# Constant products in four waits of TensorE, and three changes of order, in a two-layer diffusion step

## The reference, cut to what matters

```python
m = silu(cond) @ w_ada[l] + b_ada[l]                  # 6 vectors of 1024 per condition
h = x * (1 + m[1]) + m[0];  proj = h @ w_in[l]
s = q1 @ k1.T, q2 @ k2.T;  pd = softmax(s1) - lam * softmax(s2);  o_a = rms_norm(pd @ v)
mixed = concat([o_a, o_b, o_c])                       # 512 + 256 + 256 columns
x = layer_norm(ALPHA * x + m[2] * (mixed @ w_out[l]), ln_g[0], ln_b[0])
h = x * (1 + m[4]) + m[3]
y = moe_ffn(h)          # sigmoid router, best group, top 2 of its 4 experts; silu(h wg) * (h wu) @ wd
x = layer_norm(ALPHA * x + m[5] * y, ln_g[1], ln_b[1])
```

## Time and profile before

| | us |
|---|---|
| timed runs: median (lowest to highest) of 3 | 2076.75 (2075.97 to 2078.27) |
| the profiled execution | 2085.36 |
| its span, first to last instruction | 2083.5 |
| its mean granted TensorE clock | 0.936 of 2.4 GHz |

### The profile page before, as it was taken

The page is one execution under the profiler, slowest core; times in us unless marked ns, Lnnn a source line. Parts: engine busy times, 40 slices in busy tenths (PEclk is TensorE's granted clock), DMA queues, the critical chain, the costliest instruction groups (busy, mean ns, idle before and its releaser), DMA issues. The chain is left out here.

```text
span 2083.5 us, 20602 instructions
## 1 busy us (share of the span) xinstructions
PE 1809.4 (87%) x7528; PEld 927.7 (45%) x7528; DVE 755.3 (36%) x1179; ACT 374.4 (18%) x695; POOL 310.7 (15%) x348
## 2 busy tenths in 40 slices
PE   3999999788956999999799999988798399999983
PEld 1464555554443443434345445554545243443431
DVE  0036567374462110111060575746636310110105
ACT  1323122243010000000141422213411000000002
POOL 0001266000000000000130223630000000000005
PEclk9999999899977999999899999998998599999996
DMA  9421111565019687799603012136121696797934
GB/s 364 151 98 41 36 54 46 207 238 194 21 51 364 251 328 291 286 358 379 220 38 125 13 46 84 47 132 222 54 75 42 249 348 233 294 357 299 393 124 151
DMA packets 142086, 380.43 MB, mean 183 GB/s; under 512 B 9732, under 2 KB 15876, under 8 KB 135332
## 3 DMA queue, kind: packets, MB, share of 16 engines
q1 hardware_dynamic: 111840, 292.31, 37.5%
q10 hardware_dynamic: 21108, 55.36, 7.5%
q0 software_dynamic: 9040, 31.46, 4.1%
HBM read 343.65 MB, written 35.45 MB: 182 GB/s over the span
## 5 line engine op out<-in xcount | busy, mean ns | idle before, releaser
L855 PE MATMUL psum<-sb_arena 128*128 128x512 f32 (+1 forms) x1248 | 494.1, 596 | 10.6 <-DMA sb_arena<-w_up 9.1
L583 PE MATMUL psum<-sb_wA,sb_arena 128*128 128x512 f32 x800 | 365.3, 605 | 0.9 <-DMA sb_wA<-w_in 0.9
L855 PEld LDWEIGHTS psum<-sb_arena 128*128 128x128 f32 (+1 forms) x1248 | 192.5, 171 | 269.7 <-issue 257.7
L855 PE MATMUL psum<-sb_wA,sb_arena 128*128 128x512 f32 (+1 forms) x672 | 278.4, 611 | 9.3 <-DMA sb_wA<-w_up 6.6
L583 PEld LDWEIGHTS psum<-sb_wA,sb_arena 128*128 128x128 f32 x800 | 147.5, 192 | 165.3 <-issue 158.0
L1329 DVE TENSOR_TENSOR sb_arena<-sb_arena 128x320 f32<-128x320 f32 (+8 forms) x252 | 170.8, 719 | 13.4 <-POOL sb_arena L1264 3.8
L1849 DVE COPY sb_arena<-psum 128x1024 f32<-128x1024 f32 x32 | 39.2, 1225 | 344.3 <-PE psum L843 344.3
L855 PEld LDWEIGHTS psum<-sb_wA,sb_arena 128*128 128x128 f32 (+1 forms) x672 | 103.3, 170 | 120.2 <-issue 109.7
L1495 DVE COPY_PREDICATED sb_arena<-sb_masks,psum 128x640 f32<-128x640 uint8 x128 | 112.4, 878 | 90.8 <-PE psum L656 71.5
L574 PE MATMUL psum<-sb_arena,sb_wA 128*128 128x128 f32 (+1 forms) x512 | 140.4, 435 | 0.0
L815 PE MATMUL psum<-sb_wA,sb_arena 128*128 128x512 f32 x320 | 140.3, 599 | 0.0
(11 more groups left out here) (184 smaller groups left out, 1685.1 us busy)
## 6 DMA issues: line engine op xcount, KB each, us to landing
sb_arena<-w_gate SPq DMA_DIRECT2D x22, 2048.0 KB, 18.5
sb_arena<-w_down SPq DMA_DIRECT2D x22, 2048.0 KB, 15.8
sb_wA<-w_up SPq DMA_DIRECT2D x16, 2048.0 KB, 19.4
sb_arena<-w_up SPq DMA_DIRECT2D x16, 2048.0 KB, 15.5
sb_wA<-w_ada SPq DMA_DIRECT2D x13, 2048.0 KB, 7.7
sb_wA<-w_in SPq DMA_DIRECT2D x12, 2048.0 KB, 9.6
sb_arena<-w_ada SPq DMA_DIRECT2D x11, 2048.0 KB, 7.6
sb_wA<-w_gate SPq DMA_DIRECT2D x10, 2048.0 KB, 18.0
```

The costliest lines, as they stand in the source:

```text
L583: mm = pe.matmul(unit_bank(n), hT[:, k, t * P:(t + 1) * P], w[:, k, :], start=k == 0, stop=k == KD - 1)
L855: mm = pe.matmul(out[r, :], act_T[:, k, r], w[:, k, cs], start=k == 0, stop=k == kn - 1)
```

## The change

Four edits, in both layers unless said:

1. `HALVES`: half pieces 0 to 3 are done after the scores of heads 0 and 1 and before the wait for head 0; heads 1 to 18 have one each, head 19 the last two.
2. `stay_warm(b, n)`: n products of the identity with 512 constant columns into bank 2, whose result nobody reads: 6 before the wait for `m_ready`, 11 before `at_ready`, 8 before the first block's tokens, 5 before `pos_ready`.
3. `mix_ready` is raised once per tile. TensorE turns tiles 0 and 1 once `oa_evac` and `row_sum` are complete, tile 2 behind the projection of tile 0 and tiles 3 and 4 behind that of tile 1. ACT's three loads now stand behind the evacuation of tile 1 and a wait for all five tiles.
4. Last norm of layer 1: ACT sums x and its squares (two passes with `accum_out`), POOL computes mean, variance, power and bias in six small operations, ACT normalises, DVE multiplies by g and adds b, two tiles behind its residual. The wait for the rows g and b (`ln2_in`) moves ahead of the first tile, in both layers.

```diff
-HALVES = [range(n + (n + 1) // 5 - (n % 5 == 4), n + 1 + (n + 1) // 5) for n in range(20)]
+HALVES = [range(4)] + [range(n + 3, n + 4) for n in range(1, 19)] + [range(22, 24)]
...
+            def stay_warm(b, n):
+                for _ in range(n):
+                    pe.matmul(bank(b), ident, cst[:, 0:W], start=True, stop=True)
...
                     if n + 1 < 20:
                         scores(n + 1)
+                    if n == 0:
+                        for h_ in HALVES[0]:
+                            row_products(h_)
                     pe.wait_ge(pd_ready, nth(l, 20, n + 1))
...
-                pe.wait_ge(mix_ready, l + 1)
-                for t in range(NT):
+                def turn_mixed(t):
+                    pe.wait_ge(mix_ready, nth(l, NT, t + 1))
                     tile_transposes(NT + t, ...)
+                pe.wait_ge(oa_evac, nth(l, NT, NT))
+                pe.wait_ge(row_sum, nth(l, 3, SLABS[l]))
+                turn_mixed(0)
+                turn_mixed(1)
...
+                    for t_ in ([2], [3, 4], [], [], [])[t]:
+                        turn_mixed(t_)
                     if t >= 2:
                         router(t - 2)
...
+                stay_warm(2, 6)
                 pe.wait_ge(m_ready, l + 1)
...
+                stay_warm(2, 11)
                 pe.wait_ge(at_ready, l + 1)
...
+                stay_warm(2, 8)
                 tokens_in(0)
...
+                stay_warm(2, 5)
                 until(pe, pos_ready, l + 1)
...
                 for t in range(NT):
                     tile_evac(NT + t, hT[:, :, t * P:(t + 1) * P])
+                    if t == 1:
+                        act.wait_ge(mix_ready, nth(l, NT, NT))
+                        act.dma_start(lnb[:, 0, :], ...)    # and the two others, moved from ahead of the loop
...
+                    for t in range(NT + 1):
+                        if t < NT:
+                            act.wait_ge(last_x, t + 1)
+                            act.activation(scrap[2 * t], x[:, t, :], ACT.Copy, accum_out=sum1[:, t:t + 1])
+                            act.activation(scrap[2 * t + 1], x[:, t, :], ACT.Square, accum_out=sum2[:, t:t + 1]).then_inc(sums_ready, 1)
+                        if t:
+                            act.wait_ge(rstd_ready, nth(l, N_VAR, 2 + 2 * NT + t))
+                            act.activation(x[:, t - 1, :], x[:, t - 1, :], ACT.Identity, bias=nmr[:, t - 1:t],
+                                           scale=rstd[:, t - 1:t]).then_inc(centred, 1)
...
+                        until(gp, sums_ready, t + 1)
+                        gp.tensor_scalar(nmean[:, c1], sum1[:, c1], -1.0 / D, None, ALU.mult)
+                        gp.tensor_scalar(fine[0], sum2[:, c1], 1.0 / D, EPS, ALU.mult, ALU.add)
+                        gp.drain()
+                        gp.tensor_tensor(fine[1], nmean[:, c1], nmean[:, c1], ALU.mult)
+                        gp.drain()
+                        gp.tensor_tensor(fine[0], fine[0], fine[1], ALU.subtract)
+                        gp.drain()
+                        gp.tensor_tensor(rstd[:, c1], fine[0], mhalf[:, 0:1], ALU.pow)
+                        gp.drain()
+                        gp.tensor_tensor(nmr[:, c1], nmean[:, c1], rstd[:, c1], ALU.mult).then_inc(rstd_ready, 1)
...
-                        rms_normalised(n // 4 - 1)
+                        rms_normalised(n // 4 - 1).then_inc(mix_ready, 1)
...
                 for t in range(NT):
+                    if l + 1 == DEPTH:
+                        residual(t).then_inc(last_x, 1)
+                        if t >= 2:
+                            final(t - 2)
+                        continue
```

More of the change, by code:

```diff
@@ L275, in build_program @@
         spare = sm(OVB)
+        sum1, sum2 = Z[:, 0:NT], Z[:, NT:2 * NT]
+        fine = [cc[:, 0:1], cc[:, 1:2]]
+        scrap = [view(o_, 1024) for o_ in (0, 1024, 2048, 3072, 4096, 5120, 6144, 7168, 10240, 14592)]
         modc = sm(4 * KD).rearrange("p (m y k) -> p m y k", m=2, y=2)
@@ L300, in build_program @@
         x_in, consts, lam_in = sem("x_in"), sem("consts"), sem("lam_in")
-        cst_in, nmr_ready, mod_tr, modc_ready = sem("cst_in"), sem("nmr_ready"), sem("mod_tr"), sem("modc_ready")
+        cst_in, last_x, sums_ready, nmr_ready, mod_tr, modc_ready = sem("cst_in"), sem("last_x"), sem("sums_ready"), sem("nmr_ready"), sem("mod_tr"), sem("modc_ready")
         bias_in, cond_in, cond_zero = sem("bias_in"), sem("cond_in"), sem("cond_zero")
@@ L781, in _ @@
                         probs_v(n - 1)
-                    for h_ in HALVES[n]:
-                        row_products(h_)
+                    if n:
+                        for h_ in HALVES[n]:
+                            row_products(h_)
                 probs_v(19)
@@ L1124, in _ @@
                 act.dma_start(gate_mod[:], mod_rows(l, 2, 1)).then_inc(m2_in, 16)
[L1125 to L1128, removed]
                 for t in range(NT):
                     tile_evac(NT + t, hT[:, :, t * P:(t + 1) * P])
+                    if t == 1:
+                        act.wait_ge(mix_ready, nth(l, NT, NT))
+                        act.dma_start(lnb[:, 0, :], rows("ln_g", l * 2048, D)).then_inc(ln1_in, 16)
+                        act.dma_start(lnb[:, 1, :], rows("ln_b", l * 2048, D)).then_inc(ln1_in, 16)
+                        act.dma_start(shift2.rearrange("p y m d -> p y (m d)"), mod_rows(l, 3, 2)).then_inc(m34_in, 16)
                 for t in range(NT):
@@ L1195, in _ @@
                 if l + 1 == DEPTH:
-                    for t in range(NT):
-                        normalise(l, t)
+                    for t in range(NT + 1):
[7 more added lines that the diff above has]
+                                           scale=rstd[:, t - 1:t]).then_inc(centred, 1)
         @block.gpsimd
@@ L1312, in _ @@
                                               bass.IndirectOffsetOnAxis(ap=posi[:, t, q:q + 1], axis=0)).then_inc(cmb_in[t], 16)
[L1314 to L1321, removed]
+                if l + 1 < DEPTH:
+                    until(gp, ln2_in, l * 32 + 32)
+                    for t in range(NT):
+                        until(gp, var_ready, nth(l, N_VAR, 3 + 2 * NT + t))
+                        gp.tensor_tensor(rstd[:, t:t + 1], mv[:, t, 1:2], mhalf[:, 0:1], ALU.pow).then_inc(rstd_ready, 1)
+                else:
+                    for t in range(NT):
+                        c1 = slice(t, t + 1)
+                        until(gp, sums_ready, t + 1)
[9 more added lines that the diff above has]
+                        gp.tensor_tensor(nmr[:, c1], nmean[:, c1], rstd[:, c1], ALU.mult).then_inc(rstd_ready, 1)
         @block.vector
@@ L1879, in _, with residual, final @@
                 until(v, m5_in, l * 16 + 16)
-                for t in range(NT):
[L1881 to L1886, removed]
+                until(v, ln2_in, l * 32 + 32)
+                def residual(t):
+                    v.wait_ge(cmb_mm, nth(l, NT, t + 1))
+                    dr_()
+                    tt(ysum, psum[:, (t % 2) * 1024:(t % 2) * 1024 + 1024], gate_mod[:, 0 if t == 0 else 1, :]).then_inc(cmb_used, 1)
+                    dr_()
+                    return stt(x[:, t, :], x[:, t, :], ALPHA, ysum, ALU.mult, ALU.add)
+                def final(t):
+                    v.wait_ge(centred, nth(l, NT, t + 1))
+                    tt(x[:, t, :], x[:, t, :], lnb2[:, 0, :])
+                    dr_()
+                    tt(x[:, t, :], x[:, t, :], lnb2[:, 1, :], ALU.add).then_inc(x_ready, 1)
+                for t in range(NT):
+                    if l + 1 == DEPTH:
[3 more added lines that the diff above has]
+                        continue
+                    residual(t)
                     dr_()
@@ L1894, in _ @@
                     ts(mv[:, t, 1:2], mv[:, t, 1:2], EPS, None, ALU.add).then_inc(var_ready, 1)
[L1895 to L1899, removed]
                 if l + 1 == DEPTH:
-                    v.wait_ge(centred, nth(l, NT, NT))
-                    times_g(l, NT - 1)
+                    final(NT - 2)
+                    final(NT - 1)
 def shape_constants(np):
```

## The result

Timed beside the kernel before, the changed kernel takes 2059.31 us (2053.43 to 2066.35, 5 runs) against 2077.97: a ratio of 0.9914 (95% interval 0.9887 to 0.9941). Timed again later with the last group of experiments it was 0.9890 (0.9870 to 0.9910). It is faster, by 18 to 23 us where 33.5 were forecast. The profiled execution took 2056.94 us, its span 2055.1, its mean granted clock 0.963.

What follows compares the result with a forecast made beforehand. TensorE, busy 87% of the span, was the bound, losing time to standstills and half clock. Gains 14.0 + 11.0 + 2.0 + 6.5 = 33.5 us took profiled 2085.36 to 2051.9, forecast 2043 timed; 8-in-10 range 2034 to 2058.

Steps and rivals of the forecast that it cites:

- the one on the half pieces: Attention, wait for head 0: four half pieces moved ahead fill it, against a new load wait; 2.0 us gained in all.
- my slow end: Attention's half pieces, worst case: cold throughout and the load landing late, 4 us later per layer.
- Mixed branches: Between attention and projection: turning tile by tile starts product 0 10.15 us earlier, 3.1 given back; 14.0 us in both layers.
- Constant products: Routing waits: unread products fit inside them and raise TensorE's clock for what follows; 5.5 us a layer, 11.0 in both.
- Rival B: Routing: the clock falls again between the groups, so 3.0 us a layer, 5 less in all, 2048; chance 0.18.
- The fourth group: Five constant products ahead of the combine: cost nothing either way, with the clock expected at half again there.
- Last norm: End of layer 1: work moved from DVE to ScalarE and GpSimd, chain about 4.5 us; gain 6.5 us.
- Rival A: Last norm: GpSimd becomes the bound with chains of 8.2 us, +12.8 in place of -6.5, time 2062; chance 0.10.
- rival C: After the routing: 5.1 us a layer gained would be spent waiting for w_up, time 2053.4; chance 0.08.
- the slow clock (D): Added products never lift the clock and overrun their waits by 12.3 us a layer; sum +16, 2093; chance 0.04.
- The conversion: From profiled to timed: the profiled 2085.36 lies 8.6 us above the timed median 2076.75, so 2051.9 becomes 2043.2.
- all fast ends but the attention's: Whole kernel: every term except attention's half pieces at its fast end, given as the 2034 us low end.

Runs made afterwards that it cites:

- the pause: The changed kernel with four half pieces ahead of head 0, none at heads 1 and 2, then one each, two at heads 8, 12, 16: 2041.59 us, 0.9805.

## Why the prediction was wrong, point by point

**The step that failed** is the one on the half pieces: "half piece 4 now asks for it one head earlier in order and some 8 us after issue: a wait of up to 2 us that was not there". I had named the mechanism and mis-sized both of its times. The request came 4.7 us after the issue in layer 0 and 5.1 in layer 1. The 8 us do not follow from the costs beside them. From head 0's transpose to the half piece behind head 1 the kernel before took 2.8 us at half clock: 0.40 in the earlier trace rows, and 2.40 from the scores to the half piece here:

```profile
401.62 1.64 PE L738 MATMUL psum<-sb_arena 64*128 64x128 f32 x4
...
404.02 1.94 PE L502 MATMUL psum<-sb_wA,sb_condW 128*32 128x512 f32 x8
```

With half pieces 2 and 3 at half clock (3.9) that makes 6.7 us, and with the rise that the same paragraph takes for the four, 5.5. In the changed kernel the two half pieces took 1.9 us at full clock; the steps behind them took 2.9, no less than cold, since they now wait for ScalarE and DVE (0.37 and 0.59 above). And the landing was taken at its median of 7.6 where the range went to 13.5; beside the x copy it was 10.8. What followed I had not in the sum at all: the wait itself throws the clock down, so heads 2 and 3 ran at half after all. The term was -2.0; the traces give +9.3, the edit alone +7.9 (5.2 to 10.8). That is 10 to 11 of the 16 us. Even my slow end, 4 a layer, was short of layer 0's 6.0.

**Mixed branches, -14.0.** The mechanism was right: product 0 comes 10.4 and 10.1 us earlier after the last heads (forecast 10.15), and 3.2 are given back in layer 1 (3.1), but only 1.4 in layer 0. The traces give 15.9 in all, or 16.6 with the edit put back alone; 18.7 (13 to 24) by the times.

**Constant products, -11.0.** Right: 11.4 (5 to 18), and 11.7 by the stages of the two traces. Rival B has a share that the sum had allowed for: each group begins at half clock again (12 records in 7.49, where the earlier trace rows's rate makes 5.15; 22 in 11.34 for 9.4; 16 in 8.51 for 6.9), yet ends in time, and L850 took 2.72 against 4.47. In four of the other traces the token numbers of layer 0 stayed cold: 4.1 us from the first start to the last, against 2.1 to 2.4. The fourth group brought nothing, as said.

**Last norm, -6.5.** It gave 4.6 to 5.9. GpSimd's chains took 2.6 to 3.6 us, under the 4.5 I took, but the first 5.8 with its hole, and DVE stood 2.75 us there. My sum lets the last chain take 3.6 (2065.9 to 2069.5) and not the 4.5 that I name, without a reason; that the last one did take 3.6 is luck. Rival A did not come. A hold of GpSimd by VectorE can be seen: the 0.61 row above ends at 2033.18, as the first of DVE's two does (2031.91 + 1.23 = 2033.14), and the power took 1.36 once, 0.57 to 0.58 otherwise. The Trainium skill, "SBUF — State Buffer", section "Who interferes with whom", has it as an exclusive lock between a VectorE instruction with two SBUF inputs and a GpSimd instruction that reads SBUF; the trace agrees. That it costs so little, because DVE mostly waits for the chain that it would block, is argued and not shown.

**Weights (rival C) and the slow clock (D).** Neither: TensorE's waits for w_up are 13.7 us in the changed kernel, 15.7 in the one before, 15.6 without the constant products; they did not take up the gain.

**The conversion.** Taking 8.6 us off for the profiled run of before was sound: at the first scores, ahead of anything changed, it was 4.1 us later than the changed kernel's, as two of the others were too, and from the token numbers to the combine of layer 0 6.1 slower than the kernel that has the same code there (399.9 against 393.8). So the 28.4 us between the two profiled runs are no measure of the change; the ratios are. The four parts as measured, 15.9 to 16.6, 11.4 and 4.6 to 5.9 less 7 to 9, make 23 to 27; the ratios say 18 to 23. Of the miss of 16.3 us, 10 to 11 are the half pieces, about 1 the norm and 1.2 the kernel before, whose median was 2077.97 in the end and 2076.75 in the runs the forecast starts from; the mixed branches brought some 2 more than forecast. That leaves 4 to 8 us that are not assigned: the five runs lie 13 us apart. The low end of the range does not follow from its terms either: all fast ends but the attention's give 2037, not 2034.

## What to carry to other kernels

When work is pulled ahead of a wait, follow the buffer behind it: the load that the moved work releases is issued later relative to its next use, and every step in between must be timed at the clock that the edit itself creates. Filling a wait can pay by the clock of what follows alone, even with products that nobody reads (7.5 us here); but whether the moved work paid was decided behind it: +8 us without a pause, -13 with one that lasts until the next load has landed, each against the same kernel with the old half pieces. Sending a large copy elsewhere only moves the collision: look at what is issued next to its new place.

## What the runs showed of the hardware that was not expected

- After a wait of 3.36 us TensorE came back at half clock (scores 1.03 before it, 1.65 after). After a wait of 2.15 us it did so in some traces and not in others: the one for head 5, layer 1, stands alike in the six traces that have the pause and the x copy in its old place, and behind it the granted clock was 0.51 in the first of them and 1.00 in the one without constant products.
- That settles part of a spread that would otherwise pass for an effect of an edit. Attention of layer 1 with the pause took 97.3 us in four traces and 100.2 or 100.3 in two, with the same code. The step from head 5 to head 6 took 4.6 us in the four and 5.6 or 5.7 in the two; the rest of the difference was not traced to its place.
- Constant products in front of a long series of semaphore waits, a register load and eight empty turns of the overflow loop seem to delay these: the next product came 6.5 us after the last constant one, "issue" in both layers. That it is this series is argued from the code, not shown.
- A 2 MB load issued 4.3 us behind a 2.5 MB copy landed after 10.8 us, one issued 1.5 us behind it after 13.6, against medians of 7.5 to 8.0 in the fourteen traces.
- The hole in GpSimd's first chain of the last norm, behind a drain, was 2.95 us in nine traces, and 7.01 and 6.95 in the two where the first operations stood directly behind the ten gathers; its reason is open.
